# A two-block transformer kernel in split fp32: the remainder of a weight is made one unit later, and a pair's work is reordered on ACT and DVE

## The reference

```python
# first block: gated delta rule, then short convolution; conv_ffn in both layers
h = layer_norm(ALPHA * h + mix, ln_mix_g[i], ln_mix_b[i])
h = layer_norm(ALPHA * h + conv_ffn(h, ffn_w_up[i], ffn_conv[i], ffn_w_down[i]), ...)

def conv_ffn(h, w_up, conv_w, w_down):
    u, gate = jnp.split(h @ w_up, 2, axis=-1)
    u = causal_dwconv(u, conv_w)               # 3 taps
    return (jax.nn.silu(u) * gate) @ w_down

# second block: MLA and stick-breaking heads, then forgetting attention
x = layer_norm_2(DEEPNORM_ALPHA * x + mix, ln1_g[i], ln1_b[i])
x = layer_norm_2(DEEPNORM_ALPHA * x + swiglu(x, ffn_w1[i], ffn_w3[i], ffn_w2[i]), ...)
x = x + jax.nn.sigmoid(x @ ple_w_gate[i] + ple_b_gate[i]) * (p[i] @ ple_w_proj[i])
```

## Time and profile before

| what | value |
|---|---|
| median of 3 runs | 1779.3 us |
| profiled execution, its own time | 1794.88 us |
| its span, first to last instruction | 1793.1 us |
| mean granted clock of TensorE | 0.909 of full |
| PE busy | 1580.6 us (88%) |
| DVE busy | 1035.0 us (58%) |
| ACT busy | 972.4 us (54%) |
| POOL busy | 333.1 us (19%) |
| read from HBM | 222.86 MB, 125 GB/s over the span |

### The profile page before, as it was taken

The page is one execution under the profiler, slowest core; times in us unless marked ns, Lnnn a source line. Parts: engine busy times, 40 slices in busy tenths (PEclk is TensorE's granted clock), DMA queues, the critical chain, the costliest instruction groups (busy, mean ns, idle before and its releaser), DMA issues.

```text
span 1793.1 us, 33772 instructions
## 1 busy us (share of the span) xinstructions
PE 1580.6 (88%) x12337; PEld 1489.6 (83%) x12337; DVE 1035.0 (58%) x1675; ACT 972.4 (54%) x1588; POOL 333.1 (19%) x391
## 2 busy tenths in 40 slices
PE   7988998997796998886969878998999789998997
PEld 7965997797696988876969776898999776998997
DVE  7856223365554487655644865465646756555547
ACT  5582001255546744555467566655586577655675
POOL 2010000013111051131110510141203420232104
PEclk9997555699898999999989898999999899999999
DMA  6540000044444645444436341255565551455562
GB/s 227 167 127 5 2 1 1 1 134 129 129 141 122 194 130 166 128 135 127 139 120 195 116 141 48 71 164 164 177 176 163 156 162 48 121 170 170 162 196 97
DMA packets 62439, 225.12 MB, mean 126 GB/s; under 512 B 6928, under 2 KB 8080, under 8 KB 62352
## 3 DMA queue, kind: packets, MB, share of 16 engines
q1 hardware_dynamic: 61776, 221.87, 40.9%
q10 hardware_dynamic: 576, 2.07, 0.3%
HBM read 222.86 MB, written 1.05 MB: 125 GB/s over the span
## 4 chain that ended last, share of the span: by engine, by line
PE 48%; DVE 20%; issue 15%; ACT 13%; POOL 1%; DMA 1%; DVEq 1%; ACTq 1%; POOLq 0%; SPq 0%
PE bank L321 10%; PE bank L322 10%; PE bank L323 10%; ACT w_hi L848 7%; DVE w_lo L1296 4%; DVE av L1591 2%; PE bank L540 1%; DVE x_lo L1331 1%; DMA raw<-w 1%; PE bank L524 1%; DVE cv L1583 1%; ACT unused L835 1%; PE bank L539 1%; DVE cv L1581 1%; PE bank L472 1%
## 5 line engine op out<-in xcount | busy, mean ns | idle before, releaser
L321 PE MATMUL bank<-x_hi,w_hi 128*128 128x258 f32 (+5 forms) x2344 | 686.3, 293 | 88.3 <-DVE w_lo L1296 56.0
L322 PE MATMUL bank<-x_lo,w_hi 128*128 128x258 f32 (+5 forms) x2344 | 673.6, 287 | 0.0
L323 PE MATMUL bank<-x_hi,w_lo 128*128 128x258 f32 (+5 forms) x2344 | 673.1, 287 | 0.0
L1296 DVE TENSOR_TENSOR w_lo<-raw,w_hi 128x1024 fp32r<-128x1024 f32 x299 | 372.8, 1250 | 307.5 <-ACT w_hi L848 296.0
L321 PEld LDWEIGHTS bank<-x_hi,w_hi 128*128 128x128 f32 x2344 | 453.4, 193 | 106.4 <-issue 91.2
L322 PEld LDWEIGHTS bank<-x_lo,w_hi 128*128 128x128 f32 x2344 | 453.4, 193 | 0.7
L323 PEld LDWEIGHTS bank<-x_hi,w_lo 128*128 128x128 f32 x2344 | 453.0, 193 | 0.0
L848 ACT ACTIVATE w_hi<-raw 128x1024 fp32r<-128x1024 f32 x299 | 309.2, 1048 | 54.9 <-PE bank L323 41.8
L1294 DVE SCALAR_TENSOR_TENSOR w_lo<-raw,negmean,w_hi 128x1024 fp32r<-128x1024 f32 x120 | 154.2, 1285 | 205.5 <-ACT w_hi L846 204.9
L321 PE MATMUL bank<-a_hi,w_hi 128*128 (+2 forms) x704 | 200.4, 285 | 26.3 <-DVEq L1586 23.3
L323 PE MATMUL bank<-a_hi,w_lo 128*128 (+2 forms) x704 | 199.7, 284 | 0.0
(11 more groups left out here) (354 smaller groups left out, 2257.9 us busy)
## 6 DMA issues: line engine op xcount, KB each, us to landing
raw<-w SPq DMA_DIRECT2D x419, 512.0 KB, 3.6
h<-h SPq DMA_DIRECT2D x2, 544.0 KB, 7.1
out<-h SPq DMA_DIRECT2D x8, 128.0 KB, 1.9
con_b<-cb ACTq DMA_DIRECT2D x1, 712.0 KB, 4.2
con<-ca ACTq DMA_DIRECT2D x1, 592.0 KB, 7.2
p_raw<-pin ACTq DMA_DIRECT2D x1, 512.0 KB, 5.1
prm<-par ACTq DMA_DIRECT2D x1, 209.0 KB, 4.7
```

The source lines that it names most:

```text
L321: pe.matmul(o, wh, xh, start=first, stop=False)
L322: pe.matmul(o, wh, xl, start=False, stop=False)
L323: return pe.matmul(o, wl, xh, start=False, stop=last)
L1296: V.tensor_tensor(w_lo[:, slot, :], raw[:, slot, :], w_hi[:, slot, :].bitcast(F32), ALU.subtract).then_inc(S("lo_ready"), 1)
```

## The change

On DVE, ahead(u, s) makes the remainder of unit u+3 instead of u+4. The first remainders before the loops are one fewer, and the loop of a layer norm makes one more before the norm and one fewer after it, so that the order of the units is the same. On ACT, ahead does the split ahead of the row mean. In a pair, ACT waits for PE's unit and does its first split before it waits for tu; DVE makes its first remainder behind the bias of the convolution, and its second ahead of the read of the gate half. Between the standard deviation and the first loop of a pair phase, ACT loads the table set of SiLU.

```diff
@@ ACT
             def ahead(u, s):
+                split(u + RING, s + RING)
                 row_mean(u + (RING + 1), s + RING + 1)
-                split(u + RING, s + RING)
@@ ACT, pair
                     M = N
+                    act.wait_ge(S("unit_done"), u + 1)
+                    ahead(u, s)
                     act.wait_ge(S("ffn_tu"), jb + 1)
                     if conv is not None:
                         M = N - 2
                         A(cv[:, par, 0:M], tu[:, par, 0:M], ACT.Copy, scale=par_col(conv, j * 3)).then_inc(S("ffn_tap0"), 1)
-                        ahead(u, s)
                         act.wait_ge(S("ffn_taps"), j + (cbase + 1))
                         A(sl[:, par, 0:M], cv[:, par, 0:M], ACT.Silu, bias=wbs[:, par:par + 1]).then_inc(S("ffn_silu"), 1)
                     else:
                         A(sl[:, par, 0:M], tu[:, par, 0:M], ACT.Silu, bias=tu[:, par, N:N + 1]).then_inc(S("ffn_silu"), 1)
-                        ahead(u, s)
...
                 deviation(2 * ups[0], N)
+                act.preload_act_table_set("silu_and_others")
                 with act.Fori(0, 6) as i:
@@ DVE
             def ahead(u, s):
-                split(u + RING, s + RING)
+
+                split(u + RING - 1, s + RING - 1)
@@ DVE, layer_norm
-                for j in range(2 + RING * full, nk - 2):
+                for j in range(2 + RING * full, nk - 1):
                     ahead(u0 + j, u0 + j)
...
-                for j in range(nk - 2, nk):
-                    ahead(u0 + j, u0 + j)
+                ahead(u0 + nk - 1, u0 + nk - 1)
@@ DVE, before the loops
-            for u in range(1, RING):
+            for u in range(1, RING - 1):
                 split(u, u)
@@ DVE, pair
                     dve.sem_inc(S("acc_used"), 1)
-                    ahead(u, s)
                     if conv is not None:
...
                         V.tensor_tensor(wbs[:, par:par + 1], t[:, N:N + 1], total, ALU.mult)
+                        ahead(u, s)
                         dve.wait_ge(S("ffn_tap0"), j + (cbase + 1))
...
+                    else:
+                        ahead(u, s)
+                    ahead(u + 1, s + 1)
                     times_rstd(gate, u + 1, s + 1, N).then_inc(S("ffn_tg"), 1)
                     dve.wait_ge(S("ffn_tg"), j + (base + 1))
                     dve.sem_inc(S("acc_used"), 1)
-                    ahead(u + 1, s + 1)
                     dve.wait_ge(S("ffn_silu"), j + (base + 1))
```

## The result

| what | before | changed |
|---|---|---|
| runs, us | 1778.88 to 1781.63, median 1779.4 | 1669.90, 1674.72, 1689.60, 1693.39, median 1682.2 |
| ratio, 95% interval | | 0.945 [0.937, 0.953] |
| profiled execution, its own time | 1794.88 us | 1669.90 us |
| its span, mean granted clock | 1793.1 us, 0.909 | 1668.1 us, 0.930 |

The change makes the kernel 97 us faster. Predicted were 126.7 us and a time of 1652.6 us; 1682.2 lies just above the range of 1632 to 1680. The profiled execution's own time, predicted at 1668.2, is 1669.9, but that agreement is luck: 16.5 of its 125 us lie ahead of the first up-projection, nearly all in the gated delta rule, which the change does not touch. Without them it would be 1686.4.

What follows compares the result with a forecast made beforehand. PE was held to the pace of a chain that DVE and ACT hand to and fro. Gains 78.4 + 17.2 + 19.0 + 4.7 + 9.4, less losses 1 + 1, make 126.7 us off median 1779.3: 1652.6, range 1632 to 1680.

Steps and rivals of the forecast that it cites:

- The pair of DVE: Convolved up-projections: DVE and ACT would need 5.35 us per pair of units against PE's 5.88, so PE bounds.
- The port rival: POOL's operations hold DVE up, convolved pair 6.19 us, DVE bounds by 0.31 over PE; 1668 us, chance 0.12.
- The convolved stages: Two convolved up-projections: each falls from 166.25 to 127.0 us, gain 39.2 twice, 78.4 us.
- the wait for the sum of h: Convolved up-projections: PE's waits for POOL's sum, 25.5 us in four pieces, would end; gain inside the 78.4.
- The start of the down-projection: First unit after each convolved stage: 13.70 us becomes a unit of 2.9 and a wait of 2.2; gain 17.2.
- The unconvolved stages: Two unconvolved up-projections: each falls from 133.11 to 123.6 us, gain 9.5 twice, 19.0 us.
- b_in: The b_in stage falls from 83.47 to 74.1 us, last wait from 9.8 to 3.9; gain 9.4 us.
- The ends: Ends of the two unconvolved up-projections: gain 2.35 us twice, 4.7 us.
- The losses: 1 us lost in the kqv stage, and 1 us in the last gate stage and the attention's projections together.
- The median: Whole kernel: the 126.7 us worked out on the profiled execution was taken off the runs' median, giving 1652.6 us.
- The chain closes again: DVE waits for the tap instead of w_hi, pair stays 7.49 us; 1768 us, chance 0.08 including loads left.
- raw comes too late: Raw, requested up to a unit later, lands too late and the kernel gets slower; 1858 us, chance 0.03.

Runs made afterwards that it cites:

- experiment 7: The changed kernel run once more, unaltered: six runs of 1669.0 to 1690.1 us, median 1673.8 us, ratio 0.942 to the kernel before.

## Why the prediction came out as it did

**The mechanism** of the gain was right. DVE's wait for w_hi was replaced by no wait of that size, the 68 waits of 56.0 us became 17 of 23.4, and the later remainder alone gives all of the 97 us: distance between ACT's and DVE's step, not the order within the pair. One reading was too strong. The waits for w_lo are not most but half of the 42.8 us that up0 lost: 21.6 us, with 8.2 for the sum of h.

**The pair of DVE, 5.35 us,** is the step that failed: it was worked out from DVE and ACT alone, with 1.5 us a stage put in for POOL. Leaving POOL's work on h out made up0 8.2 us shorter (134.57 to 126.33, against 127.0 forecast). Without that work a pair is 5.6 to 5.8 us, and in one of 5.69 a remainder of 1.76 beside a_lo takes 0.54 more than one of 1.22. Take that off and 5.15 are left, so DVE's own work was sized well (5.35), and the error of this step is POOL. With POOL's work on h a pair is 6.8 us in the first three pairs and mostly 6.1 to 6.2 afterwards. So DVE stayed the slower engine against PE's 5.88. The port rival had the right mechanism and the right size of a pair (6.19), and so of a stage (127.0 + 22 x 0.31 = 133.8 us), and got a chance of 0.12. Its time, 1668, was still too low, for the other misses below. The evidence against it, a remainder of 1.23 us in a convolved stage, was read from DVE alone. In the kernel before, POOL has beside it:

```profile
405.41 1.76 POOL L1837 TENSOR_SCALAR h<-h,prm 128x262 f32<-128x262 f32 x1
```

The same operation takes 0.57 us at 395.09. So the collision was there, and POOL paid, because DVE had started at 405.20. The row of POOL at the same place would have shown it before the change.

**The convolved stages, 127.0 us,** took 134.6 and 133.3. By the terms: the short waits for remainders were 1.6 us (forecast 1.5). The start wait was 2.06 and 2.12, and behind it the matmuls of the fourth unit start over 4.17 us instead of 2.8, at the lower clock for most of that; together 3.3 against the forecast of 1.7. (In the profile of experiment 7 no lower clock follows the same wait, and up0 takes 134.28 us all the same: by this one pair of profiles that part costs nothing where DVE sets the pace.) And the wait for the sum of h, put at nothing, was 3.93 and 3.92, again with a slower unit behind it (24 matmuls over 4.5 us instead of 2.8), some 5.5 us in all:

```profile
449.25 0.98 PE L383 MATMUL bank<-hs,con 128*128 128x262 f32 x2 [3.65 <-POOLq L1854]
```

That "pair's product is there some 2 us after its second unit" held only for a DVE that keeps up.

**The start of the down-projection,** a wait of 2.2 forecast as idle time, was 3.39 and 3.53 us of idle time (3.67 and 3.81 from start to start), and its first unit took 7.76 us in place of 5.1. Here the reordering of ACT was costed at nothing: I had moved w_hi ahead of the tap, but not the row mean that belongs to the same helper. Gain 12.3 instead of 17.2.

**The unconvolved stages,** 123.6 forecast, were 125.4 and 123.2: right within 2 us, with start waits of 2.63 and 1.94 (2.2 forecast). But the account of them was incomplete: the table loads alone are worth 9 us in each. **b_in** was right: 74.07 us against 74.1, its last wait 4.05 us of idle time against 3.9. **The ends** 4.8 against 4.7. **The losses** of 2 did not come: kqv's last matmul comes 0.4 us earlier, and the first gate stage's new waits of 1.73 and 1.01 us are paid by the one ahead of f_f, 7.03 instead of 9.73.

**The median.** The forecast of what the change does was 19.2 us too good (127.7 against 108.5). The remaining 10.4 of the 29.6 us, by subtraction, are most likely the clock's: six later runs of the same kernel have a median of 1673.8 us, 8.4 below the first four. Taking the microseconds of one profiled execution off the median is sound only for executions of equal clock, and the one of before was 15.6 us above its median, that of the change 12.3 below. The lower bound of the range has a slip: 1652.6 less 15 is 1637.6, not 1636; nothing hangs on it.

**The rivals.** "The chain closes again" (1768) and "raw comes too late" (1858) are out; ACT's waits for raw ahead of a row mean fell from 13.8 to 2.6 us; those ahead of w_hi rose from 0.5 to 6.4, of 1.75 at most, since the split now comes first, so there are fewer in all. Of the list of what would show it, the loads are gone from the lines of the pair and the unconvolved stretches are as said; the pairs of 5.88 us with DVE waiting for PE, the end of the waits for the sum of h, and the stretches of 127 us did not come. The sign named for the port, a pair of over 5.9 us with DVE busy, did.

## What to carry to other kernels

Where two engines hand a chain to and fro, put one unit of distance between their steps first: this alone gave the whole gain, and shuffling the order within a pair cost some 4 us with it and, with the table loads in the loop, 38 us without it. When a faster pace of an engine is worked out, read the neighbour that shares its port in the same microseconds, and charge the engine with what that neighbour paid until now. A wait that goes on an engine which stays the slower one comes back at the next place, so cure the pace before the waits.

## What the runs showed of the hardware

- DVE and POOL hold each other up for most of an instruction, and a head start of 0.06 us decides which: remainder 1.76 and a_lo 0.74 us, or remainder 1.22 and a_lo 1.75 us.
- In the profile of the changed kernel, eight of the ten waits of 2 to 4 us that PE has at L321 and L383 were followed by a stretch at the lower level (clock 0.50 from 381.3 to 384.7, 0.51 from 449.6 to 453.0), which adds about 1.5 us to the price. Behind the waits of 2.37 us at 594.23 and 3.03 at 932.48 the clock is 1.00. The same wait at the start of up0 was followed by it in one profile of this kernel and not in the other (1.00 from 378.3 to 384.5 in experiment 7).
- The part of the gated delta rule took one of two times, about 16 us apart, with more or less of it at the lower level, in 14 profiles of kernels in which this part is the same; no kernel was seen with both.
